# Second projection of a two-block kernel: seven quarter products for ten weight blocks, feature-major queries and keys, loads a head ahead

## What is computed

```
h = x @ w_in                                   # [1024, 9216]
ua, va, za, qh, kh, vh, zb, ga, gb = split(h)  # 1024 columns each
q = rope(qh) * 64**-0.5 ; k = rope(kh)         # 8 heads x 2 halves of 64 features
pr = softmax(causal(q k^T))                    # for each half, in blocks of 128 queries
o = (pr[0] - lam * pr[1]) @ vh                 # 128 values a head
yb = rms_norm(o) * silu(zb)
merged = sigmoid(ga) * (ya @ w_a) + sigmoid(gb) * (yb @ w_b)
```

## Time and profile before

| | before |
|---|---|
| median of three runs | 2537.79 us |
| the profiled execution: its span | 2544.3 us |
| PE busy | 2425.4 us (95%) |
| DVE, ACT, POOL busy | 1172.9, 908.8, 748.5 us |
| mean granted clock of PE | 0.981 |

### The profile page before, as it was taken

How to read it: one execution, slowest core, us unless ns; L and a number is a source line. 1 busy time by engine, 2 the same in 40 slices (tenths; PEclk the granted TensorE clock), 3 DMA queues, 4 the chain that set the end, 5 groups by cost and what they waited for, 6 DMA issues and landing times.

```text
span 2544.3 us, 41785 instructions
## 1 busy us (share of the span) xinstructions
PE 2425.4 (95%) x16392; PEld 2128.2 (84%) x16392; DVE 1172.9 (46%) x2536; ACT 908.8 (36%) x1686; POOL 748.5 (29%) x725
## 2 busy tenths in 40 slices
PE   6999989999998798999999999999999999999996
PEld 5778968888787698999999889777899777787795
DVE  3001349999996333140000053454454464577535
ACT  4214554444443233131121233333333343554321
POOL 3112224545543121222213232332332332232123
PEclk9999999999999899999999999999999999999998
DMA  4323343343333422132223233133233225375611
GB/s 184 125 108 133 117 158 133 121 142 112 113 132 124 164 103 99 66 115 96 79 95 112 82 117 108 50 124 112 70 105 108 90 89 187 118 270 193 217 54 67
DMA packets 155118, 305.01 MB, mean 120 GB/s; under 512 B 11456, under 2 KB 79680, under 8 KB 143696
## 3 DMA queue, kind: packets, MB, share of 16 engines
q1 hardware_dynamic: 90704, 214.73, 24.2%
q10 hardware_dynamic: 64256, 88.10, 9.7%
HBM read 203.69 MB, written 99.09 MB: 119 GB/s over the span
## 4 chain that ended last, share of the span: by engine, by line
PE 71%; issue 14%; DVE 8%; DMA 2%; POOL 2%; ACT 2%; POOLq 0%; SPq 0%; DVEq 0%; ACTq 0%
PE bank L393 11%; PE bank L395 10%; PE bank L394 10%; PE bank L404 8%; PE bank L405 7%; PE bank L406 7%; PE bank L2087 3%; PE bank L2067 3%; POOL w_lo L359 1%; PE bank L1384 1%; PE bank L2056 1%; PE bank L676 1%; PE bank L2371 1%; DVE w_lo L359 1%; DVE rec_z L1119 1%
## 5 line engine op out<-in xcount | busy, mean ns | idle before, releaser
L404 PE MATMUL bank<-w_hi,at_hi 128*128 128x256 f32 x2432 | 705.7, 290 | 7.7 <-DVE at_lo L1584 6.8
L405 PE MATMUL bank<-w_lo,at_hi 128*128 128x256 f32 x2432 | 692.6, 285 | 0.0
L406 PE MATMUL bank<-w_hi,at_lo 128*128 128x256 f32 x2432 | 692.5, 285 | 0.0
L393 PE MATMUL bank<-at_hi,w_hi 128*128 128x512 f32 x1472 | 608.8, 414 | 5.9 <-ACT stage L429 5.5
L395 PE MATMUL bank<-at_hi,w_lo 128*128 128x512 f32 x1472 | 578.8, 393 | 0.0
L394 PE MATMUL bank<-at_lo,w_hi 128*128 128x512 f32 x1472 | 577.4, 392 | 0.0
L359 POOL TENSOR_TENSOR w_lo<-w_raw,w_hi 128x2048 fp32r<-128x2048 f32 x69 | 318.2, 4611 | 843.3 <-ACT w_hi L372 843.3
L404 PEld LDWEIGHTS bank<-w_hi,at_hi 128*128 128x128 f32 x2432 | 471.7, 194 | 20.9 <-issue 12.0
L405 PEld LDWEIGHTS bank<-w_lo,at_hi 128*128 128x128 f32 x2432 | 471.0, 194 | 0.8 <-issue 0.2
L406 PEld LDWEIGHTS bank<-w_hi,at_lo 128*128 128x128 f32 x2432 | 470.5, 193 | 0.0
L429 ACT ACTIVATE stage<-bank 128x512 f32<-128x512 f32 x272 | 161.9, 595 | 623.4 <-PE bank L395 320.0
(11 more groups left out here) (256 smaller groups left out, 2958.3 us busy)
## 6 DMA issues: line engine op xcount, KB each, us to landing
w_raw<-in_weights SPq DMA_DIRECT2D x84, 1024.0 KB, 7.0
feat<-stage ACTq DMA_DIRECT2D x152, 256.0 KB, 2.0
tok<-stage ACTq DMA_DIRECT2D x104, 256.0 KB, 2.2
stage<-feat SPq DMA_DIRECT2D x32, 256.0 KB, 3.5
x<-in_x SPq DMA_DIRECT2D x4, 1024.0 KB, 9.6
w_mem<-in_w_mem SPq DMA_DIRECT2D x4, 1024.0 KB, 11.5
logg<-gate_g ACTq DMA_DIRECT2D x8, 512.0 KB, 2.8
rec_b<-logg SPq DMA_DIRECT2D x16, 256.0 KB, 5.2
```

The lines of the kernel that those rows point to most:

```text
L393: nc.tensor.matmul(ps_gemm[i % 2], wh, ah, start=(k == 0), stop=False)
L404: nc.tensor.matmul(o, ah, wh, start=(k == 0), stop=False)
L405: nc.tensor.matmul(o, ah, wl, start=False, stop=False)
L406: last = nc.tensor.matmul(o, al, wh, start=False, stop=(k == KT - 1))
```

## The change

The last three steps of phase 5 and the form of queries and keys are replaced.

* Phase 5 now starts with the four "T" blocks of the values. Then come ten blocks (four of queries, four of keys, two of gates), all feature-major, by Strassen's scheme: each weight block is stored as four corners (512 rows by 128 columns), the activations are taken as four quarters (512 features by 512 tokens), and the 2x2 product is formed from seven quarter products of 12 matmuls each, where the plain form has eight. Two plain "F" blocks of gates follow.
* The activations' four sums and differences (`t1` to `t4`) are formed by DVE once and split in hi and lo by ACT and DVE. For each block DVE forms three sums of corners (`weight_sums`) and replaces the fourth corner in `w_raw`; ACT and POOL split corners and sums.
* The seven products go to the two banks in turn. Partial results are kept in `xu` and `stage`; ACT does the two that are pure copies, DVE the five that add a bank to something.
* Queries and keys lie feature-major in memory. Each is loaded twice, once as it is, once with the groups of 32 features swapped (four strips of 32 rows); rotation is then `x*cos + swapped*sin` with tables 1024 columns wide and the sign in the table. The transposes and the copies to `dqT`, `dkT` are gone; scores read `dqx`, `dkx`, two buffers.
* Constants, tables, and the first loads of head 0 stand behind the quarter blocks, beside the two plain ones. Values and gates have two buffers; those of the next head are issued by ACT in the fourth query block of the head before.
* `first_scores`: the scores of a head's first query block are formed before the last slot of the head before. DVE's loop over heads is unrolled.

The core of the diff:

```diff
-        gemm2 = [
-            Segment(8, "T", ACT.Copy, tok2, QH),
-            Segment(4, "T", ACT.Copy, tok2, VH),
-            Segment(4, "F", ACT.Silu, feat2, ZB),
-        ]
+        gemm2 = [Segment(4, "T", ACT.Copy, tok2, VH)]
+        gemm_quarters = [
+            Segment(4, "F", ACT.Copy, feat2, QF),
+            Segment(4, "F", ACT.Copy, feat2, KF),
+            Segment(2, "F", ACT.Silu, feat2, ZB),
+        ]
+        gemm_before = [Segment(2, "F", ACT.Silu, feat2, ZB + 2 * CB)]
...
+        def quarter_product(pe, bank, left, right, start):
+            (wh, wl), (ah, al) = left, right
+            for k in range(QUARTER):
+                c = slice(k * P, (k + 1) * P)
+                nc.tensor.matmul(bank, wh[:, c], ah[:, k, :], start=(start and k == 0), stop=False, skip_group_check=True)
+                nc.tensor.matmul(bank, wh[:, c], al[:, k, :], start=False, stop=False, skip_group_check=True)
+                last = nc.tensor.matmul(bank, wl[:, c], ah[:, k, :], start=False, stop=(k == QUARTER - 1), skip_group_check=True)
+            return last
...
+        def quarter_block(pe, m):
...
+            pe.wait_ge(w_split, g + 3)
+            if m:
+                pe.wait_ge(q_dve, 5 * m + 1)
...
+            quarter_product(pe, even, l11, r11, True).then_inc(q_done, 1)
+            if m:
+                pe.wait_ge(q_dve, 5 * m + 2)
...
+            quarter_product(pe, odd, s2, t2, True).then_inc(q_done, 1)
+            pe.wait_ge(q_act, 2 * m + 1)
+            quarter_product(pe, even, l12, r21, False).then_inc(q_done, 1)
+            pe.wait_ge(q_dve, 5 * m + 3)
+            quarter_product(pe, odd, s3, t3, True).then_inc(q_done, 1)
+            pe.wait_ge(q_act, 2 * m + 2)
+            quarter_product(pe, even, s1, t1, True).then_inc(q_done, 1)
+            pe.wait_ge(q_dve, 5 * m + 4)
...
+            quarter_product(pe, odd, l22, t4, False).then_inc(q_done, 1)
+            pe.wait_ge(q_dve, 5 * m + 5)
+            last = quarter_product(pe, even, s4, r22, False)
...
+        def weight_sums(dve, m):
...
+            dve.wait_ge(w_loaded[b], ((Q_AT + m) // 2 + 1) * 16)
+            if m:
+                dve.wait_ge(w_split, Q_AT + m + 2)
+            link(dve, nc.vector.tensor_tensor(xs[:, 0, :], raw[3], raw[2], ALU.add))
+            nc.vector.tensor_tensor(raw[3], raw[0], raw[3], ALU.subtract)
+            link(dve, nc.vector.tensor_tensor(xs[:, 1, :], xs[:, 0, :], raw[0], ALU.subtract))
+            nc.vector.tensor_tensor(xs[:, 2, :], raw[1], xs[:, 1, :], ALU.subtract).then_inc(q_sums, 1)
...
+        def weight_lows(pool, m):
+            b, g = m % 2, Q_AT + m
+            pool.wait_ge(w_high, g + 1)
+            pool.tensor_tensor(wx_lo[b][:], xs[:], wx_hi[b][:].bitcast(F32), ALU.subtract)
+            split_low(pool, g // 2, b)
...
+        def quarter_results(act, m):
+            b, func = m % 2, Q_BLOCKS[m][0].func
+            if m < Q_N - 1:
+                sums_high(act, m + 1)
+            act.wait_ge(q_done, PRODUCTS * m + 1)
...
+            nc.scalar.activation(xu[:, b, :], ps_gemm[b], ACT.Copy).then_inc(q_act, 1)
+            if m < Q_N - 1:
+                loaded_high(act, m + 1)
...
+            act.wait_ge(q_done, PRODUCTS * m + 3)
+            corner_free(act, m, 0)
+            nc.scalar.activation(stage[:, 0, :], ps_gemm[b], func).then_inc(q_act, 1)
...
+        def quarter_sums(dve, m):
...
+            nc.vector.tensor_tensor(u, odd, u, ALU.add).then_inc(q_dve, 1)
+            dve.wait_ge(q_done, PRODUCTS * m + 4)
...
+            nc.vector.tensor_tensor(stage[:, 3, :], odd, u, ALU.add).then_inc(q_dve, 1)
+            dve.wait_ge(q_done, PRODUCTS * m + 5)
...
+            nc.vector.tensor_tensor(stage[:, 3, :], even, stage[:, 3, :], ALU.add).then_inc(q_dve, 1)
+            if m + 2 < Q_N:
+                weight_sums(dve, m + 2)
+            dve.wait_ge(q_done, PRODUCTS * m + 6)
...
+            nc.vector.tensor_tensor(stage[:, 2, :], odd, u, ALU.add).then_inc(q_dve, 1)
+            block_products_done(dve, m)
...
+            last = nc.vector.tensor_tensor(stage[:, 1, :], even, u, ALU.add)
...
         def p5_sp(sp):
+            for segs in (gemm2, gemm_quarters):
+                gemm_sp(sp, segs)
+            sp.wait_ge(tile_done, ALL_QUARTERS + 8)
+            for to, of in ((dposi, I["positions"].partition_broadcast(P)), (dfr, I["freq"]),
...
             queries_load(sp, 0)
-            gemm_sp(sp, gemm2[2:])
+            all_stored(sp, gemm_quarters)
+            values_load(sp, 0)
+            gemm_sp(sp, gemm_before)
...
         def queries_load(sp, head):
...
+            for x, swapped, at, done in ((dqx[head % 2], dqs, QF + row, d_in), (dkx[head % 2], dks, KF + row, d_in)):
+                sp.dma_start(x[:], feat2[at:at + P, :]).then_inc(done, 16)
+                for n in range(4):
+                    other = at + (n ^ 1) * 32
+                    sp.dma_start(swapped[n * 32:(n + 1) * 32, :], feat2[other:other + 32, :]).then_inc(done, 16)
...
+        def rope_third(eng, x, swapped, ready, done, head, third):
+            to = x[head % 2]
             if third == 0:
+                eng.wait_ge(ready, 160 * (head + 1))
+                eng.tensor_tensor(to[:], to[:], dcos[:], ALU.mult).then_inc(done, 1)
             elif third == 1:
+                eng.tensor_tensor(swapped[:], swapped[:], dsin[:], ALU.mult).then_inc(done, 1)
             else:
+                eng.wait_ge(done, 3 * head + 2)
+                eng.tensor_tensor(to[:], to[:], swapped[:], ALU.add).then_inc(done, 1)
...
         def p5_dve(dve):
             normed_low(dve, 1)
+            quarter_differences(dve)
+            weight_sums(dve, 0)
+            weight_sums(dve, 1)
+            for m in range(Q_N):
+                quarter_sums(dve, m)
             dve.wait_ge(consts_in, 48 + 48)
...
+                if it < B_HEADS - 1 and qb == 3:
+                    act.wait_ge(d_o, it * 8 + 1)
+                    act.wait_ge(d_y, it * 8 + 1)
+                    values_load(act, it + 1)
...
         def head_pe(pe, it):
-            pe.wait_ge(d_e, it * 16 + 2)
-            for x, ps, done, ready in ((dq, ps_a, d_tq, d_rq), (dk, ps_b, d_tk, d_rk)):
-                pe.wait_ge(ready, it * 6 + 6)
-                for t in range(NT):
-                    last = nc.tensor.transpose(ps[:, t // 4, (t % 4) * P:(t % 4 + 1) * P],
-                                               x[:, t].rearrange("p m a n -> p (m a n)"), ident[:])
-                last.then_inc(done, 1)
             slot_products(pe, it, FIRST_SLOT)
-            pe.wait_ge(d_eq, it + 2)
-            pe.wait_ge(d_ek, it + 2)
-            attention_scores(pe, it, 0)
...
+            if it < B_HEADS - 1:
+                first_scores(pe, it + 1)
             slot_products(pe, it, LAST_SLOT)
             outputs_transpose(pe, it, NT - 1)
```

More of the change, by code:

```diff
@@ L113, in build @@
         stage = sb("stage", [P, SLOTS, HALF])
+        with ExitStack() as own:
+            t4_lo = sb("t4_lo", [P, QUARTER, HALF], F32R, own)
         fill = sb("fill", [P, 2, TOK])
@@ L207, in build @@
             daT = sb("da_aT", [P, NT, P], F32, own)
-            dg = sb("da_gate", [P, TOK], F32, own)
+            dg = [sb(f"da_gate{n}", [P, TOK], F32, own) for n in range(2)]
             dy = sb("da_y", [P, TOK], F32, own)
@@ L1677, in p4_pool, with quarter @@
             split_low(pool, gemm_out[1][1].first // 2 + 1, 1)
+        Q_AT = gemm_quarters[0].first
+        Q_BLOCKS = [(s, n // 2, n % 2) for s in gemm_quarters for n in range(s.n)]
+        Q_N = len(Q_BLOCKS)
+        assert Q_AT % 2 == 0
+        q_done, q_act = sem("q_done"), sem("q_act")
+        q_dve = credited("q_dve", "dve", 2)
+        q_sums = sem("q_sums")
+        ALL_QUARTERS = 4 * (Q_AT + Q_N)
+        CORNERS = ((0, 0), (0, 1), (1, 0), (1, 1))
+        def quarter(x, kh, h):
+            return x[:, kh * QUARTER:(kh + 1) * QUARTER, half(h)]
@@ L1680, in p5_pe, with differences_high @@
+        def differences_high(act, which):
+            for n in which:
+                raw, hi = ((1, t1_hi), (0, t3_hi), (2, t2_hi), (1, t4_hi))[n]
+                act.wait_ge(fill_tp, 4 * KT + n + 1)
+                nc.scalar.activation(hi[:], xr[:, raw], ACT.Copy).then_inc(fill_hi, 1)
         def p5_pe(pe):
@@ L1879, in p5_dve @@
             link(dve, nc.vector.tensor_scalar(dlam[:, 6:7], cols[:, SUBG:SUBG + 1], 1.0 - LAM_INIT, None, ALU.mult))
[L1880 removed]
+            rope(dve, dqx, dqs, d_in, d_rq, 0)
         def p8_dve(dve):
[L1883 to L1885 removed]
+            for head in range(B_HEADS):
+                head_dve(dve, head, head == B_HEADS - 1)
         def head_dve(dve, it, last_head):
[L1888 to L1889 removed]
             scores_max(dve, it, 0)
@@ L2086, in attention_scores @@
                     w = min(HALF, n - a)
-                    last = nc.tensor.matmul(scored(ps, qb)[:, a:a + w], dqT[rows, qb * P:(qb + 1) * P], dkT[rows, a:a + w],
```

(2 more changed lines are left out.)

336 lines of the change are left out of this document (232 added, 104 removed).

## The result

| | before | after |
|---|---|---|
| median | 2539.06 us (4 runs, 2536.48 to 2541.07) | 2493.36 us (4 runs, 2489.87 to 2497.34) |
| profiled execution: span | 2544.3 us | 2495.5 us |
| mean granted clock of PE | 0.981 | 0.979 |

The ratio is 0.982, with an interval of 0.9804 to 0.9835: 45.7 us between the medians. A longer series of the same program later gave 2489.98 us (5 runs) against 2539.51 (8 runs), ratio 0.9806 [0.9792, 0.982], 49.5 us. The two profiled spans differ by 48.8 us, and that is the number to take apart; the forecast was 51.6. The order of reading is that of the earlier trace rows: page, stage windows, block spacing, then the chain in a head.

The account below looks back on a forecast made before the run. PE was taken as the bound, so its instruction count and spacing decide. Projection 36.7 us (10.4 + 27.2 - 0.9), heads 12.3 and head 0's start 2.6 sum to 51.6 us saved: forecast 2486.2 us, range 2478 to 2503.

Parts of the forecast that it names:

- behind head 7: Stretch from the last head's end to the end of the execution: no change, 0 us.
- Orientation: Second projection: eight query and key blocks become feature-major, 21.75 us each for 23.05, saving 10.4 us.
- Seven products: Ten quarter blocks: 84 matmuls of 512 columns for 96, 19.03 us a block, saving 27.2 us.
- pause at each change of product: Rival, quarter blocks: first matmul of a product 0.2 us slower at 70 changes, 14 us, 2500 us; chance 0.08.
- exposed wait: First tile of the two plain blocks waits for tile_out, raised by DVE after the last product: 0.9 us lost.
- DVE's queue: Quarter blocks: 1.0 us of slack, no cost; rival: late weight sums cost 1 to 2 us a block, 2494 to 2502; chance 0.12.
- series rival: Quarter blocks: weights' preparation begins only after product 5, block 28.5 us, ten cost 95 us more, 2581; chance 0.04.
- The fourth difference's copy: ACT's copy in the projection delays an evacuation from 1142.2 to 1146, PE asks at 1147.9: no cost.
- Tables: Plain blocks, Q the quarter blocks' end: table work covered, no cost; rival: ACT holds a bank, up to 5 us; chance 0.05.
- Rope in the heads: Rival: POOL's rotation delays da up to 2.9 us against 2.2 of cover, 0.7 us in seven heads, 2491; chance 0.10.
- Head 0: From projection's end to da in the first head: 12.3 us instead of 14.9, saving 2.6 us.
- the transposes' term: Heads 1 to 7: sixteen transposes of queries and keys removed, 1.75 us a head, saving 12.3 us.

Follow-up runs that it names:

- experiment 1: Kernel after with its ten quarter blocks as plain feature-major blocks of 96 matmuls, no weight sums or activation differences: 2519.41 us, ratio 0.9911 to before.
- experiment 3: Kernel after with four unused DVE additions of 448 columns behind the weight sums in eight quarter blocks: 2495.55 us, blocks of 20.65 us.
- experiment 2: Kernel after with each quarter product cut from 12 matmuls to 9, part of the computation missing, other engines unchanged: 2459.67 us, blocks of 16.7 us.
- experiment 5: Kernel after with sixteen transposes of queries and keys put back at each head's start, results unread: 2506.22 us, ratio 0.9864 to before.
- experiment 6: Kernel after with tile_out raised earlier for 39 of forty tiles, and heads 1 to 7's first scores back directly before the second: 2486.43 us, ratio 0.979 to before.
- after_again: The kernel after, unchanged, run as a second series: 2489.98 us (5 runs).
- experiment 7: Kernel after with values and gates fetched at each head's own start: 2496.73 us, repeated 2490.49; with SP's last-head loads held until they landed, 2488.08.

## Why the prediction held, and where it was off

**The form of the argument held.** PE is the bound before and after; each piece of PE time that the change removes came back in full, and no rival took any of it. Of the difference 1.8 us is PE time that the change adds, and 1.2 is no property of the kernel (behind head 7, below). The forecast 2486.2 lies 7.2 us under the first median and 3.8 under the second; the span fell by 48.8 us for 51.6. So 2.8 of the 7.2 are the forecast's own; the rest is the medians' spread, which includes that of the 2537.79 it starts from.

**Orientation:** 10.4 us forecast, 10.4 measured (experiment 1). **Seven products:** 27.2 forecast, 27.0 measured; the block takes 19.04 us for 19.03. Matmuls of 512 columns keep their 226.7 ns from start to start across changes of bank and of operands: the pause at each change of product isn't there. By the 215.7 ns of the Trainium skill (TensorE: Matmul & The Clock Gate, part 1, "Wait — 56ns, not 53.3ns?") an estimate of the block would be 18.1 us. The trace doesn't agree: the block is 19.04.

**The exposed wait** ahead of the plain blocks: forecast 0.9, measured 0.9 (the wait for stage L1887 above), and 1.1 from the last quarter matmul's slot to the first plain one. Taking it away gave 1.2 us.

**DVE's queue:** 1.0 us of cover forecast, 1.3 measured, because linked additions of 512 columns follow one another at 0.6 to 0.7 us, which makes the four 2.7 for 2.9 and the sum of product 6 behind them 0.6 for 0.7. POOL's lows end at 1283.05, 1.0 ahead of their use (forecast 0.8). The rival at 0.12 didn't happen, but experiment 3 shows that it was 1.3 us away, and how it would have looked. The series rival at 0.04 took the preparation to begin after product 5, at 28.5 us a block; experiment 2 shows the series that there is, 16.7 us.

**The fourth difference's copy** on ACT delays an evacuation to 1145.34 (forecast 1146, asked for at 1147.9): nothing lost.

**Tables.** Timelines of after in the plain blocks, ACT's, then DVE's and POOL's:

```profile
1409.88 1.04 ACT L2237 ACTIVATE da_cos<-da_cos 128x1024 f32<-128x1024 f32 x1
...
1411.88 1.28 ACT L2239 ACT_TABLE_LOAD   x1
...
1414.69 0.60 ACT L444 ACTIVATE stage<-bank 128x512 f32<-128x512 f32 x1
1417.88 0.60 ACT L444 ACTIVATE stage<-bank 128x512 f32<-128x512 f32 x1 [2.58 <-PE bank L410]
...
1415.09 3.01 DVE L2070 TENSOR_TENSOR da_q<-da_q,da_cos 128x1024 f32<-128x1024 f32 x1
1418.03 3.41 DVE L2072 TENSOR_TENSOR da_qs<-da_qs,da_sin 128x1024 f32<-128x1024 f32 x1
...
1416.96 3.39 POOL L2072 TENSOR_TENSOR da_ks<-da_ks,da_sin 128x1024 f32<-128x1024 f32 x1
```

With Q at 1384.9 the held bank is out at Q + 30.4 (forecast Q + 32.7), 2.6 us ahead of the next evacuation at 1417.88, near which PE asks: the trace shows two table loads, not three, and none in front of the sines. The rotation does run in turns, each piece of 3.0 to 3.4 us where it has 1.3 on DVE or 2.4 on POOL for itself, and ends at 1424.8, 3.9 ahead of PE's last matmul. Both are ahead of need. The loads come to 3.6 MB by their sizes in the trace, 4.6 with the weight block behind them, where the forecast has 4.5; they were in time too.

**Rope in the heads.** The lock of the earlier trace rows shows again and in more places than I saw. Timelines of after in its third head, POOL's, DVE's and PE's:

```profile
1649.82 3.33 POOL L2070 TENSOR_TENSOR da_k<-da_k,da_cos 128x1024 f32<-128x1024 f32 x1
...
1648.09 2.85 DVE L2072 TENSOR_TENSOR da_qs<-da_qs,da_sin 128x1024 f32<-128x1024 f32 x1
1650.86 0.34 DVE L2190 SCALAR_TENSOR_TENSOR da_y<-bank,da_lam,da_gate 128x128 f32<-128x128 f32 x1
...
1651.31 1.86 DVE L2152 TENSOR_TENSOR small<-small,da_lam 128x1 f32<-128x1 f32 x1
...
1653.79 0.89 DVE L2157 SCALAR_TENSOR_TENSOR da_a<-da_p,small 128x640 f32<-128x640 f32 x1
...
1657.07 0.60 PE L2327 MATMUL bank<-ident,da_a 128*128 128x128 f32 x4
```

A product of one column with two SBUF operands waits 1.86 us for POOL's rotation, while the gating pass beside it, with a bank as operand, keeps 0.34. So `da` is late, at 1654.7; its transposes start at 1657.07. 2.4 us of cover are left, and the rival's 0.7 a head didn't come. The mechanism was right, its price covered.

**Head 0:** 2.6 forecast, 2.8 measured; PE's wait of 0.8 us there for the first `da`, which before has, is in no list of after.

**The step that was off: the transposes' term, 12.3 us, of which 10.4 arrived.** The transposes themselves gave their 1.75 us a head (experiment 5). What the sum lacked was the cost of `first_scores`, which the prediction credited in head 0 and left at nothing in heads 1 to 7: it splits one visit to the 64-row scores into two, and the second visit costs 0.40 us, 2.8 in seven heads (experiment 6, where PE has no other wait in the heads than in after). The row needed was in the earlier trace rows, the 0.43 for 0.23; I used it for a rival in the projection, where nothing of the kind happens, and not where the change really adds such a passage. That is more than the 1.8 us missing: with one passage the heads are 0.14 us each shorter than those of before less 1.75 (634.0 against 635.0). These 1.0 us are in no wait of either list; where they come from stays open.

**Behind head 7:** 0 forecast, +1.2 measured. PE's wait of 1.1 us for `at_lo` at L2034 stands there, which before has not (it has one of 0.6 for ACT's stage, after one of 0.7). It is a matter of the single execution. In the profile of the same program in after_again that wait is missing and the stretch takes 341.3 us, as in before; over the profiles of all the changed kernels the wait lies between 0 and 1.1 and the stretch between 341.2 and 342.5. The two executions of after differ in one load: where the wait is, ACT has stood 1.5 us until 2163.05 for `fill` to land (L2028), and in the other not at all, though SP issues the loads for the next phase 82.6 us ahead of head 7's last product in both. So the forecast of 0 stands; why that load lands later in some executions stays open.

## What to carry over

Where one engine is busy through a stage, count its instructions, take their spacing from a long row of equal steps, and each such term holds to a few tenths; then go through the changed order for each new neighbour of two unlike kinds of matmul and price it as well. A prefetch that does nothing in six rounds may be needed in the seventh, so look at the round in which another queue's work changes. When a change removes a wait, ask what that wait had kept apart. Before a small difference is explained, look at the same stretch in a second execution of the same program: here 1.2 us came and went between two of them.

## What the runs showed of the hardware

- Split into two visits, PE's matmuls for the scores (64 rows) between those of the weights (128 rows) cost 0.40 us more a head, 2.80 in seven heads (experiment 6 against after).
- PE's matmuls of 512 columns, one weight load each, start every 226.7 ns at clock 1.00, over eight blocks without a break, whichever bank or operand comes next.
- A wait of PE loses about 0.3 us more than the list gives it (blocks of 20.65 for 19.04 + 1.3, and of 16.7 for 14.3 + 2.15); half of that is where the list starts a wait, and the first matmul behind it is followed after 0.31 us for 0.23.
- Behind waits of 3.1 and 3.5 us PE ran at the lower level of its clock, weight matmuls 0.43 us apart for 0.23, which cost another 1.7 and 3.2 us (experiment 7). In experiment 2 the same came once behind a wait of 2.05 us, and not behind the other seven, of 1.9 to 2.3.
- While POOL runs a two-operand SBUF pass, even a DVE product of 128x1 waits (1.86 us). An int32 cast of 128x1024 that starts beside POOL's split ended 0.55 us after it in the kernel after and in that of experiment 1, and took 2.20 and 1.84 us. Passes with a PSUM operand keep their time (0.34 us for 128x128).
- Loads of 512 KB that land in 5.1 us alone take 15.2 and 15.7 when another queue issues 4 MB at the same moment.
